# Output projection in split passes by column halves, gate mix summed in PSUM

## Reference

```
gates = sigmoid(xn @ w_gate + b_gate).reshape(B, S, 3, D)
merged = (gates[:, :, 0] * (y_attn @ w_proj_attn)
          + gates[:, :, 1] * (y_pool @ w_proj_pool)
          + gates[:, :, 2] * (y_mem @ w_proj_mem))
h = h + merged @ w_out
h = h + moe(rmsnorm(h, norm_ffn_g), w_router, b_router, w_up, b_up, w_down, b_down)
```

## Time and profile before

| | |
|---|---|
| median of 3 runs | 1206.98 us (1204.16 to 1207.64) |
| profiled execution: its own time | 1203.21 us |
| its span in the trace | 1201.0 us |
| TensorE busy | 1121.9 us, 93% |
| VectorE, ScalarE, GpSimd busy | 359.7, 227.3, 128.6 us |
| DMA | 444.22 MB, 370 GB/s over the span |

### The profile page before, as it was taken

One profiled execution on the slowest core, in us unless ns is written; L12 is line 12 of the kernel. 1 busy time (PEld: TensorE's weight loads), 2 busy tenths in 40 slices (PEclk: granted clock), 3 DMA queues, 4 the chain that ended last, 5 costly groups with the idle time before them and its releaser, 6 DMA issues.

```text
span 1201.0 us, 14123 instructions
## 1 busy us (share of the span) xinstructions
PE 1121.9 (93%) x5609; PEld 510.0 (42%) x5609; DVE 359.7 (30%) x766; ACT 227.3 (19%) x415; POOL 128.6 (11%) x59
## 2 busy tenths in 40 slices
PE   6899999999999999999999989999989899989996
PEld 5788898753333333333333323333323233333332
DVE  4593664632222222122222222222212122222222
ACT  5354454121111111111111111111111111111112
POOL 5562666400000000000000000000000000000000
PEclk9999999989999999999999999999999999999999
DMA  9554335779999999999999999999999999999993
GB/s 355 194 177 145 113 141 188 276 310 403 384 428 427 428 427 426 427 427 430 427 427 427 427 427 427 428 428 427 429 428 427 427 427 427 427 427 427 428 426 142
DMA packets 50230, 444.22 MB, mean 370 GB/s; under 512 B 6094, under 2 KB 9592, under 8 KB 25592
## 3 DMA queue, kind: packets, MB, share of 16 engines
q1 hardware_dynamic: 48256, 441.64, 88.5%
q10 hardware_dynamic: 1912, 1.66, 0.5%
HBM read 441.65 MB, written 1.05 MB: 369 GB/s over the span
## 4 chain that ended last, share of the span: by engine, by line
PE 61%; DMA 28%; DVE 6%; ACT 3%; issue 1%; POOL 0%; SPq 0%; DVEq 0%; ACTq 0%
PE psum L1476 23%; PE psum L1512 14%; DMA ring<-in_w_up 14%; PE psum L1177 11%; DMA gm_area<-in_w_up 10%; DMA my_area<-in_w_up 4%; PE psum L1431 3%; PE psum L1364 2%; DVE gate_area L1110 1%; DVE gate_area L1114 1%; DVE gate_area L1108 1%; PE psum L1499 1%; ACT gate_area L770 1%; PE psum L1485 1%; PE psum L1220 1%
## 5 line engine op out<-in xcount | busy, mean ns | idle before, releaser
L1476 PE MATMUL psum<-ring,gate_area 128*64 128x512 f32 x1216 | 280.0, 604 | 21.7 <-DMA ring<-in_w_up 13.4
L1080 DVE TENSOR_TENSOR h_s<-psum,h_s 128x512 f32<-128x512 f32 x132 | 82.0, 684 | 426.0 <-PE psum L1431 426.0
L1476 PEld LDWEIGHTS psum<-ring,gate_area 128*64 128x64 f32 x1216 | 85.8, 139 | 203.9 <-issue 173.3
L1512 PE MATMUL psum<-ring,gate_area 128*64 128x512 f32 x640 | 145.8, 595 | 5.3 <-ACT gate_area L770 5.3
L535 POOL TENSOR_TENSOR unit_lo<-ring,unit_hi 128x1024 fp32r<-128x1024 f32 (+1 forms) x54 | 128.2, 2380 | 95.3 <-ACT unit_hi L568 95.2
L764 ACT ACTIVATE gate_area<-gate_area 128x512 f32<-128x512 f32 x32 | 20.1, 630 | 532.0 <-DVE gate_area L1106 532.0
L1106 DVE TENSOR_SCALAR gate_area<-psum 128x512 f32<-128x512 f32 x32 | 22.1, 692 | 277.1 <-PE psum L1485 277.1
L1512 PEld LDWEIGHTS psum<-ring,gate_area 128*64 128x64 f32 x640 | 44.3, 136 | 86.3 <-issue 76.3
L1476 PE MATMUL psum<-gm_area,gate_area 128*64 128x512 f32 x256 | 60.3, 609 | 6.4 <-DMA gm_area<-in_w_up 6.4
L1431 PE MATMUL psum<-pT_s,gate_area 64*128 64x512 f32 x264 | 65.6, 615 | 0.7 <-ACT pT_s L774 0.7
L568 ACT ACTIVATE unit_hi<-ring 128x1024 fp32r<-128x1024 f32 (+1 forms) x54 | 55.5, 1032 | 47.6 <-PE psum L1177 47.4
(11 more groups left out here) (244 smaller groups left out, 1180.3 us busy)
## 6 DMA issues: line engine op xcount, KB each, us to landing
ring<-in_w_up SPq DMA_DIRECT2D x76, 2048.0 KB, 37.1
ring<-in_w_down SPq DMA_DIRECT2D x40, 2048.0 KB, 38.2
qe_area<-in_w_up SPq DMA_DIRECT2D x16, 2048.0 KB, 36.8
gm_area<-in_w_up SPq DMA_DIRECT2D x16, 2048.0 KB, 39.9
my_area<-in_w_up SPq DMA_DIRECT2D x12, 2048.0 KB, 35.2
xv_area<-in_w_up SPq DMA_DIRECT2D x8, 2048.0 KB, 37.9
xv_area<-in_w_down SPq DMA_DIRECT2D x8, 2048.0 KB, 38.7
my_area<-in_w_down SPq DMA_DIRECT2D x8, 2048.0 KB, 43.6
```

The costliest lines, as they stand in the source:

```text
L1080: nc.vector.tensor_tensor(h_s[:, b, cols], psum[:, BACK_BANKS[j], :], h_s[:, b, cols], ALU.add).then_inc(added, 1)
L1476: ins = nc.tensor.matmul(psum[lo:lo + SLOTS, c, :], lhsT, w[:, at:at + 512], start=(k == 0), stop=False)
L1512: ins = nc.tensor.matmul(psum[c * SLOTS:(c + 1) * SLOTS, DOWN_BANK, :], lhsT, w[:, at:at + 512], start=(f == 0), stop=(f == KC - 1))
```

## The change

The output projection becomes split passes too. Eight units are added, four for each column half of `w_out`: unit j holds two k-chunks (k = 2j, 2j+1) of 512 columns. `out_unit` multiplies both token halves by a unit, so both results of a column half are finished in its last unit. `merged` is kept as a rounded part (`merged_hi`, copied by ScalarE from PSUM) and a remainder (`merged_lo`, VectorE). The weighted sum of the branches is written back into PSUM. The first three added units use the old unit slots, the other five get three areas of their own over the gates and other dead data.

```
+UNITS += [(f"O{hf}", "rows", j) for hf in range(2) for j in range(KC // 2)]
...
+for _f in range(KC):
+    for _n in range(3):
+        EMPTIED["br", _f, _n] = _f + 1
...
+EARLY_O = 3
+UNIT_BEFORE = {u: u - UNIT_SLOTS for u in range(UNIT_SLOTS, O_UNIT + EARLY_O)}
+UNIT_BEFORE |= {u: u - UNIT_SLOTS for u in range(O_UNIT + 2 * EARLY_O, len(UNITS))}
...
-            sp.wait_ge(bank_filled, FILLED["br", KC - 1, 2])
+            sp.wait_ge(got_parts, 24 * 16)
+            sp.wait_ge(merged_lo_ready, KC)
+            load(1, 1, 7)
+            sp.wait_ge(lo_ready, LAST_SPLIT["O0"])
+            load_over("O0")
+            sp.wait_ge(unit_used, unit_read(O_UNIT + EARLY_O - 1)[1])
             for q in range(4, 6):
                 load(0, q, q)
-            sp.wait_ge(got_parts, 24 * 16)
-            sp.wait_ge(merged_ready, KC)
-            load(1, 1, 7)
-            for name in ("O0", "O1"):
-                sp.wait_ge(bank_filled, LAST_USE[name])
-                load_over(name)
+            sp.wait_ge(lo_ready, LAST_SPLIT["O1"])
+            load_over("O1")
...
-            act.dma_start(gf_bc, norm_final_g.to_broadcast([P, D])).then_inc(got_late, 16)
             act.dma_start(g2_bc, norm_ffn_g.to_broadcast([P, D])).then_inc(got_late, 16)
-            for u in range(22 + 3 * KC + UNIT_SLOTS, len(UNITS)):
+            for f in range(KC):
+                split(P_UNIT + UNIT_SLOTS + f)
+                act.wait_ge(merged_ready, f + 1)
+                nc.scalar.activation(merged_hi[:, f, :], bank(("br", f, 0))[:, 0:S], ACT.Copy)\
+                  .then_inc(merged_hi_ready, 1)
+            act.dma_start(wr_s, rows(w_router[0])).then_inc(got_router, 16)
+            act.wait_ge(merged_lo_ready, KC)
+            for u in range(O_UNIT + EARLY_O, len(UNITS)):
                 split(u)
...
+            def take_merged_lo(f):
+                dve.wait_ge(merged_hi_ready, f + 1)
+                nc.vector.tensor_tensor(merged_lo[f], bank(("br", f, 0))[:, 0:S], merged_hi[:, f, :].bitcast(F32),
+                                        ALU.subtract).then_inc(merged_lo_ready, 1)
+
             for f in range(KC):
+                t = []
                 for i in range(3):
...
+                    if i == 1:
+                        link(ins)
+                        nc.vector.tensor_tensor(mix_t[:, 1, :], t[0], mix_t[:, 0, :], ALU.add)
+                link(ins)
+                nc.vector.tensor_tensor(t[0], t[2], mix_t[:, 1, :], ALU.add).then_inc(merged_ready, 1)
+                if f > 0:
+                    take_merged_lo(f - 1)
+            take_merged_lo(KC - 1)
...
-            def project_out(b, hf):
-                t = fill(("out", b, hf))
...
+            def out_unit(t, hf, j):
+
+                hi, lo = next_unit()
+                for b in range(B):
+                    for i in range(2):
+                        k = 2 * j + i
+                        if hf == 0 and b == 0:
+                            pe.wait_ge(merged_lo_ready, k + 1)
+                        s = slice(b * P, (b + 1) * P)
+                        ins = three_passes(t[b], (merged_hi[:, k, s], merged_lo[k][:, s]), (hi[:, i, :], lo[:, i, :]),
+                                           k == 0, k == KC - 1)
+                    if j == KC // 2 - 1:
+                        done(ins)
+                if j < KC // 2 - 1:
+                    ins.then_inc(unit_used, 1)
```

More of the change, by code:

```diff
@@ L98 @@
 UNITS += [("P", "cols", f) for f in range(D // P)]
+UNITS += [(f"O{hf}", "rows", j) for hf in range(2) for j in range(KC // 2)]
+P_UNIT = UNITS.index(("P", "cols", 0))
+O_UNIT = UNITS.index(("O0", "rows", 0))
 assert FRONT.index("PPM") == FRONT.index("PA") + 1 and FRONT.index("PA") % RING_SLOTS < RING_SLOTS - 1
@@ L129, in psum_jobs @@
     for f in range(KC):
[L130 to L133, removed]
+        jobs += [(("br", f, i), "mix") for i in range(3)]
+    jobs += [(("out", 0, 0), "dve"), (("out", 1, 0), "dve")]
+    jobs += [(("x2T", 0, 0), "act"), (("x2T", 1, 0), "act")]
+    jobs += [(("out", 0, 1), "dve"), (("out", 1, 1), "dve")]
+    jobs += [(("x2T", 0, 1), "act"), (("x2T", 1, 1), "act"), ("logits", "dve")]
     jobs += [("pos", "dve"), ("total", "dve")]
@@ L280, in hybrid_layer_kernel @@
                    "mem": (xn_parts[:, 6:8, :], memT_parts[:, 6:8, :])}
-        merged = view(xT_area, 0, KC, S)
+        merged_hi = xT_hi
+        lo_first = at("merged_lo_first", [P, KC // 2, S], pT_at, F32R)
+        lo_second = at("merged_lo_second", [P, KC // 2, S], yT_at + 4 * 4 * S, F32R)
+        merged_lo = [(lo_first if f < KC // 2 else lo_second)[:, f % (KC // 2), :] for f in range(KC)]
+        out_hi = [at(f"out_hi{i}", [P, UNIT_W], where, F32R) for i, where in enumerate((gm_at, gm_at + 8 * UNIT_W, ib_at))]
+        out_lo = [at(f"out_lo{i}", [P, UNIT_W], where, F32R)
+                  for i, where in enumerate((gm_at + 4 * UNIT_W, gm_at + 12 * UNIT_W, xT_at + 4 * (KC * S + UNIT_W)))]
         u_s = view(misc, 0, B, G * HD)
@@ L336, in hybrid_layer_kernel @@
         dve_emptied = sem("dve_emptied")
-        emptied = {"act": act_emptied, "dve": dve_emptied}
+        merged_hi_ready = sem("merged_hi_ready")
+        merged_lo_ready = sem("merged_lo_ready")
+        emptied = {"act": act_emptied, "dve": dve_emptied, "mix": merged_lo_ready}
         ones_set = sem("ones_set")
@@ L1353, in _ @@
                     done(ins)
-            n0 = block_arrived(pe, "O0")
-            n1 = block_arrived(pe, "O1")
-            def project_out(b, hf):
-                t = fill(("out", b, hf))
[L1360 to L1366, removed]
+            def out_unit(t, hf, j):
+                hi, lo = next_unit()
+                for b in range(B):
+                    for i in range(2):
[7 more added lines that the diff above has]
+                        done(ins)
+                if j < KC // 2 - 1:
+                    ins.then_inc(unit_used, 1)
             def turn_h(b, hf):
                 t = fill(("x2T", b, hf))
-                pe.wait_ge(scaled, 2 * B + 2 * b + hf + 1)
+                pe.wait_ge(scaled, 2 * B + 2 * hf + b + 1)
                 for c in range(4):
@@ L1374, in turn_h, with logits @@
                 done(ins)
-            project_out(0, 0)
-            project_out(0, 1)
-            project_out(1, 0)
+            def logits(b, hf):
+                pe.wait_ge(act_emptied, EMPTIED["x2T", b, hf])
+                for k in range(4 * hf, 4 * hf + 4):
+                    ins = nc.tensor.matmul(t_logits[:, b * NE:(b + 1) * NE], x2T[:, k, b * P:(b + 1) * P], wr_s[:, k, :],
+                                           start=(b == 0 and k == 0), stop=(b == B - 1 and k == KC - 1))
+                return ins
+            t = [fill(("out", b, 0)) for b in range(B)]
+            for j in range(KC // 2):
+                out_unit(t, 0, j)
+            t = [fill(("out", b, 1)) for b in range(B)]
+            out_unit(t, 1, 0)
+            out_unit(t, 1, 1)
             turn_h(0, 0)
-            turn_h(0, 1)
-            project_out(1, 1)
+            turn_h(1, 0)
+            out_unit(t, 1, 2)
+            out_unit(t, 1, 3)
             t_logits = fill("logits")
             pe.wait_ge(got_router, 16)
[L1385 to L1393, removed]
+            logits(0, 0)
+            logits(1, 0)
+            turn_h(0, 1)
             turn_h(1, 1)
-            done(logits(1))
+            logits(0, 1)
+            done(logits(1, 1))
             t = fill("pos")
```

59 lines of the change are left out of this document (31 added, 28 removed).

## The result

The changed kernel takes 1216.05 us (median of 4 runs) against 1205.57 us before (median of 4 too; the 1206.98 above is of three of them); the ratio is 1.0099, 95% interval 1.0067 to 1.013. Forecast was 1202.6, with 0.05 for slower. Its profiled execution took 1215.82 us, span 1214.0.

The account below looks back on a forecast made before the run. The expert loop was taken as bound by its weights' DMA, the end following the first expert matmul. Passes -4.8 and tail +0.4 gave -4.4 us, from 1206.98 to 1202.6, range 1197.5 to 1207.

Parts of the forecast that it names:

- Transfers: Expert pieces in the queue's new order: all ten land by 271.5, needed by 275.8; hidden, with 4 us of cover.
- the rest up to T0 is unchanged: Between the tail's router matmuls and the first expert matmul (T0): no change in time.
- Earlier transfers are worth nothing: Expert pieces issued sooner in the front: no gain, since the ten places are full anyway.
- the slower one: Rival in the merge: GpSimd holds up VectorE also with one input in PSUM; +1.9 us, 1209; chance 0.04.
- The end follows the first expert matmul: Whole kernel: end is first expert matmul (T0) plus a constant, if the first ten pieces land by T0 + 5.7.
- Passes: Output projection: 96 split matmuls take 22.6 us instead of 27.48, a gain of 4.8 us (3.8 to 5.3).
- Feeding: ScalarE and GpSimd splitting units for the projection: nothing waits, by 2.1 us or more.
- Merge: Mixing of branches: six VectorE instructions take 2.76 us a chunk against TensorE's 2.91; cost 0, range up to 2 us.
- just closes: Merge's longest path, from the second bank: ends at 210.80 against the next chunk's first bank at 210.74.
- The outputs' second steps among GpSimd's units: `xn2` of column half 0 among units six to eight: each held up to 2.4 us; cost 0, 1.4 cover.
- Pieces: First ten expert pieces: the tenth, slot 9, lands at 271.5, needed by first expert matmul (T0) + 5.7 = 275.8.
- Tail: Last product to last router matmul: 6.1 to 7.0 us against 6.3, taken as a loss of 0.4.

Follow-up runs that it names:

- the version with the early load: Changed kernel with ScalarE issuing the router weights' transfer behind the norm gain's, near 205 us instead of near 230: 1198.24 us, ratio 0.9948 to the kernel before.

## Why the prediction was wrong, by its steps

**The step that failed** is "Transfers", and with it "the rest up to T0 is unchanged" in the tail. I followed the ten expert pieces through the new order and found them in time, which they were. I did not follow one more transfer of that stretch, the router's load, although the prediction names the moved load of the last gain. It was put at nothing without a reason, and it cost a wait of 16.2 us, with 2.7 us of low clock behind it. Its row with 21.1 us for 128 KB stood in the transfers' table of the kernel before, and the pause of the stream behind the idle stretch from 252 to 258, which I used to show that transfers had room, was what let it land at 252.4. "Earlier transfers are worth nothing" was true and not enough: they can cost. None of the rivals was this one; the slower one named another mechanism, which the changed kernel does not show.

The 13.35 us of the first expert matmul split up as follows: last product 5.45 us sooner (257.52 to 252.07), 16.2 of waiting, 2.7 more from the end of the wait to the last router matmul (9.0 against 6.3), 0.1 less behind it. -5.45 + 16.2 + 2.7 - 0.1 = 13.35. With TensorE kept busy through the wait the first expert matmul is 3.0 us sooner, which fits the 2.7.

**The end follows the first expert matmul**: right to 1 us, with one exception. 925.6 to 926.5 us lie between it and the end in the kernel before, in the changed one and in the versions whose first ten pieces had landed in time, but 924.2 in the one with 23 more matmuls. Where the pieces had not landed, it was 931.3 and 931.6, as the condition said.

**Passes**: right in mechanism, small in size. Forecast 22.6 us, measured 96 x 0.228 = 21.9. The rows that I took the pace from ran at 0.228 us in their middle as well. Their means are longer since the first and the last record count for more and, in the 48 of 11.84 us, the first five ran at a granted clock of 0.50 (41.6 to 43.5 us). "At full pace" was a wrong reading.

**Feeding**: right; TensorE waits for no unit. **Merge**: right, 23.3 us as before. The path that "just closes" did not close by its own numbers, 210.80 against 210.74. It fits in the run, with 0.15 us of idle time of VectorE a chunk, since a multiplication that waits for no result follows at 0.35 us (208.99 to 209.34) and not at 0.46. Writing PSUM costs next to nothing (424 against 421 ns), and the hold-up of instructions with two SBUF inputs is real and larger than thought. The outputs' second steps among GpSimd's units: one of four took 0.82 instead of 0.69, hidden as reckoned. **Pieces**: in the version with the early load slot 9, the tenth, lands at 274.5 where 271.5 was reckoned, 0.7 us ahead of the limit of T0 + 5.7.

**Tail**: forecast 0.4 longer, measured 0.7 shorter with the early load (16.4 against 17.0). Up to the last router matmul it is 5.9 us against 6.3, where 6.7 was forecast: the copies end 4.7 behind the last product and not 5.0, and the 8 records run at 2.4 GHz in 1.09 us, while the sum had them half-way to 1.2 GHz. Behind it 0.2 more is gained; the low clock lasts 6.8 us there (259.9 to 266.7) and lasted 10.2 before (262.0 to 272.2). With the wait out of the way the whole front is 6.2 us shorter from the start of the merge to the first expert matmul, where 4.4 was forecast, and the time 6.3 us by the ratio (0.5%). So the term for the gain was of the right size, a little low, and the loss came from what stood in no term.

## What to carry to other kernels

When a change closes a gap in a busy DMA stream, list every transfer that is in flight in that stretch, small ones first, with its issue, its landing and its first use; one that lands as the gap begins is living on it. A transfer of many small packets beside a stream of large ones on another queue moves at one small packet per large one: issue it before the stream, put it into the stream's queue, or lay it out in larger pieces. And a VectorE instruction on a loop of waits should have at most one SBUF input while GpSimd works, since a hold-up there can repeat with each turn, as it did here.

## What was not expected of the hardware

A load of 128 KB took 37.8 us beside the stream, 4.5 us ahead of it, 9.3 us beside it with 1 KB packets. TensorE's clock was at 1.2 GHz for 30.7 us, from 255.1, 3 us into the stand of 16 us, to 285.8. Work that nothing reads, in the gaps, kept it at 2.4 GHz and paid: with 23 extra matmuls the ratio to the kernel before went from 0.9948 to 0.992, and the first expert matmul came 2.2 us sooner after the last product.
